# Where tile 0's second routing exponential stands among ScalarE's copies of two projections

## The reference, cut to what matters

```python
z = h @ w_in                                   # 2048 -> 3632 columns: q, three kv groups, gates, pooling rows
q = rms_norm(q, g_qnorm); ...                  # keys of two groups normed too
x1 = x + gate1 * mix_out(nsa(q, ...), pool_mix(u, ...), w_out)
h2 = modulate(x1, ...)
# PEER, for each token and each of 8 heads:
s1, i1 = top_k(s[:, :, 0], 16); s2, i2 = top_k(s[:, :, 1], 16)
sc, j = top_k(s1[..., :, None] + s2[..., None, :], 16)       # 16 of 256 pairs
eid = i1[j // 16] * 128 + i2[j % 16]
g = softmax(sc)
a = gelu(sum(h2 * peer_u[eid]))                # 128 gathered rows of 2048 a token
y = sum(g * a * peer_v[eid])                   # 128 more
out = x1 + gate2 * y
```

## Time and profile before

| | |
|---|---|
| three runs | 2568.68, 2570.46, 2578.82 us; median 2570.46 |
| the profiled execution | 2574.56 us, its span 2572.8 us |
| mean granted TensorE clock of the span | 0.699 |
| instructions | 17754 |
| bytes moved by DMA | 944.49 MB, 367 GB/s over the span |

### The profile page before, as it was taken

The page is one execution under the profiler, slowest core; times in us unless marked ns, Lnnn a source line. Parts: engine busy times, 40 slices in busy tenths (PEclk is TensorE's granted clock), DMA queues, the critical chain, the costliest instruction groups (busy, mean ns, idle before and its releaser), DMA issues.

```text
span 2572.8 us, 17754 instructions
## 1 busy us (share of the span) xinstructions
PE 1280.7 (50%) x6315; PEld 697.2 (27%) x6317; DVE 1757.6 (68%) x2243; ACT 212.5 (8%) x559; POOL 1184.3 (46%) x686
## 2 busy tenths in 40 slices
PE   5699998897490543266884972000015655200000
PEld 2363534482240432143331960000002222000000
DVE  1010112217967977897557667999999998899898
ACT  3110012100001221121001010000000000000000
POOL 1000100002426744575222415678876767788684
PEclk9799898899795655556995985555556677655555
DMA  9949899659999999999998989999999999999897
GB/s 299 332 172 422 324 414 291 208 196 360 388 422 397 377 366 341 405 410 370 344 373 321 414 318 410 366 393 422 422 407 407 400 420 417 417 422 422 366 422 307
DMA packets 163042, 944.49 MB, mean 367 GB/s; under 512 B 34635, under 2 KB 44435, under 8 KB 56830
## 3 DMA queue, kind: packets, MB, share of 16 engines
q0 software_dynamic: 94784, 682.66, 66.0%
q1 hardware_dynamic: 68175, 260.74, 28.2%
HBM read 937.36 MB, written 10.26 MB: 368 GB/s over the span
## 4 chain that ended last, share of the span: by engine, by line
PE 27%; DMA 25%; DVE 20%; POOL 15%; issue 9%; SPq 2%; ACT 1%; POOLq 0%; another core or an unknown queue 0%; DVEq 0%; ACTq 0%
POOL arena L668 11%; DMA arena<-in_peer_u,arena 10%; DMA arena<-in_peer_v,arena 9%; DVE arena L1975 8%; POOL arena L680 4%; DVE arena L1998 4%; DMA arena<-in_w_out 4%; PE PS L1468 3%; PE PS L1445 3%; PE PS L1016 3%; DMA arena<-in_w_ada 3%; PE PS L1166 2%; PE PS L1253 2%; PE PS L966 2%; PE PS L1423 2%
## 5 line engine op out<-in xcount | busy, mean ns | idle before, releaser
L668 POOL DMA_INDIRECT arena<-in_peer_u,arena x256 | 471.7, 1843 | 446.1 <-DVE arena L1975 240.8
L1975 DVE CUSTOM_DVE_ANT_0 arena<-arena 128x2048 f32<-128x2048 f32 x256 | 581.5, 2289 | 118.0 <-DMA arena<-in_peer_u,arena 116.7
L1998 DVE SCALAR_TENSOR_TENSOR arena<-arena 128x2048 f32<-128x2048 f32 x226 | 531.1, 2350 | 136.6 <-DMA arena<-in_peer_v,arena 131.9
L668 POOL DMA_INDIRECT arena<-in_peer_v,arena x256 | 428.3, 1673 | 369.7 <-DVE arena L1998 242.7
L1468 PE MATMUL PS<-arena 128*128 128x512 f32 x240 | 180.3, 921 | 449.9 <-DMA arena<-in_peer_v,arena 449.9
L1468 PEld LDWEIGHTS PS<-arena 128*128 128x128 f32 x240 | 69.5, 304 | 561.4 <-issue 555.1
L1474 PE MATMUL PS<-arena 128*64 128x512 f32 x8 | 5.5, 849 | 346.4 <-DVEq L2041 346.4
L2031 DVE SCALAR_TENSOR_TENSOR arena<-arena 128x2048 f32<-128x2048 f32 x64 | 150.6, 2352 | 10.8 <-DMA arena<-in_peer_v,arena 5.3
L966 PE MATMUL PS<-arena 128*32 128x512 f32 x768 | 119.4, 721 | 69.9 <-DMA arena<-in_w_ada 66.6
L2028 DVE CUSTOM_DVE_ANT_0 arena<-arena 128x2048 f32<-128x2048 f32 x64 | 145.0, 2291 | 8.4 <-DMA arena<-in_peer_u,arena 6.5
L680 POOL DMA_INDIRECT arena<-in_peer_v,arena x64 | 126.4, 1975 | 39.0 <-issue 18.6
(11 more groups left out here) (347 smaller groups left out, 1824.5 us busy)
## 6 DMA issues: line engine op xcount, KB each, us to landing
arena<-in_w_ada SPq DMA_DIRECT2D x96, 1024.0 KB, 12.1
arena<-in_w_in SPq DMA_DIRECT2D x32, 1048.0 KB, 9.2
arena<-in_peer_wq SPq DMA_DIRECT2D x32, 1024.0 KB, 10.2
arena<-in_w_in SPq DMA_DIRECT2D x32, 768.0 KB, 11.2
arena<-in_w_out SPq DMA_DIRECT2D x16, 1024.0 KB, 30.0
arena<-in_w_out SPq DMA_DIRECT2D x32, 512.0 KB, 24.0
arena<-in_peer_u,arena POOLq DMA_INDIRECT x320, 13.9
arena<-in_peer_v,arena POOLq DMA_INDIRECT x320, 15.5
```

Source lines behind the costliest of these rows:

```text
L668: pool.indirect_dma_start(out=rows_ring[:, k % NROW, :], out_offset=None, in_=tables[kind], in_offset=bass.IndirectOffsetOnAxis(ap=ids[:, ...
L1975: V.tensor_tensor_reduce(out=buf, in0=buf, in1=h2(t), scale=1.0, scalar=0.0, op0=ALU.mult, op1=ALU.add, accum_out=dots[:, t, r:r + 1]).the ...
L1998: V.scalar_tensor_tensor(out=acc[t], in0=rows_ring[:, k % NROW, :], scalar=dots[:, t, r:r + 1], in1=acc[t], op0=ALU.mult, op1=ALU.add).the ...
```

## The change

`expert_exp` gets the half as an argument. The first half of tile 0 stays where it was. The second half, with its wait for `s_e2` 2, moves behind the square root of L846, that is, behind the copies of both projections. Tiles 1 and 2 have both halves where they were.

```diff
-            def expert_exp(t):
-                for half in range(2):
-                    w = gw[:, t, half * HH:(half + 1) * HH]
-                    act.wait_ge(s_e2, 2 * t + half + 1)
-                    A(w, w, exp).then_inc(s_e2x, 1)
+            def expert_exp(t, half):
+                w = gw[:, t, half * HH:(half + 1) * HH]
+                act.wait_ge(s_e2, 2 * t + half + 1)
+                A(w, w, exp).then_inc(s_e2x, 1)
...
-            expert_exp(0)
+            expert_exp(0, 0)
 
             used(act, "ia", NK - 1, 1)
             for n in range(2):
...
             act.wait_ge(s_zms, 4)
             A(qkr[:, 1:3, NH:24], qkr[:, 1:3, NH:24], sqrt).then_inc(s_zrt, 1)
+            expert_exp(0, 1)
 
             act.wait_ge(s_qt, 2)
...
-            expert_exp(1)
+            expert_exp(1, 0)
+            expert_exp(1, 1)
             gelu(1)
-            expert_exp(2)
+            expert_exp(2, 0)
+            expert_exp(2, 1)
```

## The result

| | before | after |
|---|---|---|
| median of 20 runs, us | 2569.51 (2562.43 to 2578.82) | 2575.69 (2571.24 to 2582.13) |
| profiled execution, its span, us | 2574.56, 2572.8 | 2573.35, 2571.5 |

What follows compares the result with a forecast made beforehand. The loop over gathered rows was taken to set the pace, with DMA or VectorE late in turn. A filled DMA hole (4.3 us) plus a vanished table load (1.3) gave 5.6 off 2570.46: 2564.9 us, range 2557 to 2576.

Steps and rivals of the forecast that it cites:

- What bounds it, and what moves: Gathered-row loop sets the pace; second projection 43 us earlier is worth zero, early pieces cost rows 9 to 22 11.6 us, repaid.
- The hole from 670 to 690: DMA time left empty at 670 to 690 us gets filled by early projection pieces: 3.4 to 5.2 us gained, 4.3 taken.
- nothing is won: The 5 us DMA hole merely moves beside rows 34 to 45, as VectorE's side work fills the ring: 2570.5 us, chance 0.26.
- the 4.3 us of the sum: Gain forecast from filling the empty DMA time at 670 to 690 us, the middle of 3.4 to 5.2 us.
- New holes: VectorE's side work beside rows 34 to 41 might open DMA holes: costed at nothing, up to 9.5 us if uncovered.
- The table loads: Moved exponential's load after L846 is hidden; the load at L867 vanishes, gaining 1.3 us (bounds 0 and 1.3).
- The slower rival: Rows 9 to 22 never regain 11.6 us and 9.5 us of side work lies bare: 2587.3 us, chance 0.05.

Runs made afterwards that it cites:

- the nine gaps: VectorE waits for its own dot product to end behind rows 40 to 48 of tile 0: in the changed kernel 2566.17 us, in the kernel before 2569.48 us.
- The kernel with TensorE held: The changed kernel, with TensorE starting the second projection only after VectorE made the second half's logits: 2570.27 us, ratio 0.9999 to the kernel before.

## Why the prediction was wrong

**What bounds it, and what moves.** Right. TensorE's 43 us bought nothing as TensorE time: its next wait grew from 71.01 to 120.0 us (114 forecast). The pieces came early, and rows 9 to 22 took (701.36 - 640.78) / 13 = 4.66 us each, not 3.63 (4.52 forecast). Row 22 started 14.1 us late counted from row 0 (102.82 against 88.68), where 11.6 was forecast; that its start of 701.36 lies so near the 703 of the forecast is luck, since this execution reached row 0 4.2 us earlier. (The forecast's 703 is 691.42 + 11.6, a start; the text calls it an end.)

**The hole from 670 to 690.** Right for the place: it is full after the change (422 GB/s from 666 to 686). What that is worth once the new hole is gone is seen from the nine gaps in the two kernels: 0.9979 with the change, 0.9995 without it, a difference of 0.0016 or 4.1 us, against the 5.6 I had summed. With intervals of 0.001 on each side it is uncertain by some 4 us, and the medians alone (2566.17 of 2569.95 for the kernel before on that chip, 2569.48 of 2572.36 on the other) give only 1 us. The traces say why it may be small. I estimate the empty DMA time from 30 to 300 us after row 0, in windows of 10 us and by the rate against 423 GB/s: 15.5 us without the change and with the gaps, 13.5 with the change and with the gaps. The 5.2 us hole was filled, but part of it opened again at 130 to 180 us after row 0 (396, 356, 410, 412 and 335 GB/s), as the rival "nothing is won" had it. So the 4.3 us of the sum were not shown; 2 us is what this pair of traces bears out.

**New holes.** This is the step that failed: "so I cost them at nothing; uncovered they cost up to 9.5 us". I had the place, beside and behind rows 34 to 41, and reasoned that the ring starts empty there and that the biases and pooling weights are still in the queue. Neither held long enough. The last of these loads was issued by 739, and at row 41 the ring was full: GpSimd had waited 1.79 us for VectorE to free a slot before the held issue, and VectorE then ran five products without waiting for a row. Above all the price was not that of a full ring. A full ring should empty the DMA only until the next slot is free. What happened was one issue held 12.73 us while the DMA ran empty, 9.7 + 1.6 = 11.3 us of DMA time, more than twice the 5.2 us hole that it replaced. The difference, 6.1 us, is close to the 6.2 us between the medians, but these are two holes of many. By the estimate over 270 us, as above, the empty DMA time is 16.8 us before and 21.4 after, 4.7 more, and row 60 starts 5.1 us late. So the term put at nothing measured 11.3 us at its own place, above the 9.5 that I had given as its most.

**The warning that I passed over.** The kernel before shows two such issues, of 6.08 us at 768.60 and 7.17 us at 845.07, ending 0.85 us after the start of a row product (773.83) and 0.87 us after that of an addition with one operand in PSUM (851.37). The prediction asks only who waited, not why an issue that mostly takes 0.9 to 3 us took 7.

**The table loads.** Right in place, not shown in time. There are 18 loads in the span before and 18 after. The moved one stands behind L845's square root, with 8.64 us to spare before the next copy; the exponential of L867 has none ahead of it, and VectorE's first reduction of that branch no longer waits for it:

```profile
834.88 0.22 ACT L845 ACTIVATE arena<-arena 128x16 f32<-128x16 f32 x1 [69.00 <-DVE arena L1556]
835.11 1.28 ACT L813 ACT_TABLE_LOAD   x1
836.40 0.26 ACT L813 ACTIVATE arena<-arena 128x64 f32<-128x64 f32 x1
845.31 1.08 ACT L850 ACTIVATE arena<-PS 128x512 f32<-128x512 f32 x2 [8.64 <-PE PS L1135]
...
875.66 0.40 ACT L867 ACTIVATE arena<-arena 128x240 f32<-128x240 f32 x1
```

```profile
877.70 0.39 DVE L1632 TENSOR_REDUCE arena<-arena 128x16 f32<-128x240 f32 x1
```

It came 279.2 us after row 0 against 274.8 before, 4.4 later instead of 5.6 earlier. The kernel with TensorE held has this gain without the early pieces: its trace has this reduction 273.2 us after row 0, 1.6 earlier than before, and it measures 0.9999, whose interval holds 1.3 us off as well as nothing.

**The rivals.** "Nothing is won" named the right place, "the 5 us open beside rows 34 to 45", with half the size and another cause, a full ring. The slower rival had the pieces unpaid; they were repaid: with the hold gone, row 24 is 19.9 us late (113.37 against 93.52) and row 60 2.8 us early.

**What stays open.** Why some issues are kept out past several boundaries, while others, with the same start 0.35 us after a VectorE instruction's, get in at the next. Also how far the length of a hold differs between executions: each kernel has one trace.

## What to carry to other kernels

When a stall is removed and its transfers come earlier, look at the place that they leave: what they covered there lies bare, and it need not cost what it looks like. Read the durations of the issuing instructions, not only the waits: an indirect DMA issue on GpSimd that lasts several times its usual time beside a row of two-input VectorE instructions is a held issue. Look then at the DMA in that window: if no other queue has work, the hold can cost. A wait of VectorE for its own last instruction, 0.1 us, or a load from another engine's queue placed at that point, removed the cost here. Gaps at a hold during which the DMA was busy anyway gave nothing that could be measured.

## What the runs showed of the hardware

An indirect DMA issue on GpSimd lasted 6 to 12.7 us in some runs of VectorE products of two SBUF operands at 2.21 us intervals, and ended 0.8 to 0.9 us after the first gap (0.04 us sufficed) or, in one trace, the start of a one-input sum. Beside other such runs it took 1.9 to 2.9 us and ended 0.9 us after the start of the next product (699.66 and 881.56 before the change). With VectorE idle or in a one-input instruction it took 0.94 us. A gap after a row product of 2.29 us cost 0.12 us (2.33 between starts in place of 2.21). During the hold of 12.73 us the DMA fell to 14 GB/s although VectorE, the consumer, was never idle in the first eight microseconds of that window (776 to 784).
